# A two-block transformer kernel on one core: other places for the first weights, the turned input and the modulation groups in the opening order

## The reference, cut to what matters

```python
c_act = jax.nn.silu(c)
mod = (c_act @ ada_w[l] + ada_b[l]).reshape(B, N_MOD, D)[:, :, None, :]
shift_m, scale_m, gate_m, shift_f, scale_f, gate_f = [mod[:, i] for i in range(N_MOD)]
h = rmsnorm(x, norm_mix_g[l]) * (1.0 + scale_m) + shift_m
...
(p_q, p_k, p_v, p_g, p_gk, p_cq, p_ckv, p_kr, p_ga, p_gb) = jnp.split(h @ w_in, idx, axis=-1)
```

## Time and profile before

| | |
|---|---|
| three timed runs | 2636.22, 2636.57, 2638.76 us; median 2636.57 us |
| profiled execution, first to last instruction | span 2637.0 us |
| PE busy | 2552.6 us, 97% of the span |
| DVE busy | 1699.4 us, 64% |
| ACT busy | 1281.6 us, 49% |
| read from HBM | 549.83 MB |

### The profile page before, as it was taken

How to read it: one execution, slowest core, us unless ns; L and a number is a source line. 1 busy time by engine, 2 the same in 40 slices (tenths; PEclk the granted TensorE clock), 3 DMA queues, 4 the chain that set the end, 5 groups by cost and what they waited for, 6 DMA issues and landing times.

```text
span 2637.0 us, 33987 instructions
## 1 busy us (share of the span) xinstructions
PE 2552.6 (97%) x12327; PEld 2145.5 (81%) x12327; DVE 1699.4 (64%) x2194; ACT 1281.6 (49%) x1824; POOL 63.1 (2%) x102
## 2 busy tenths in 40 slices
PE   3889999999999999999999999999999999999999
PEld 3878887888887887888888888889888887888887
DVE  6887776776676765566655545565666655676664
ACT  3345455444555444544443444455754545565553
POOL 0000000000000000000000000000000100010000
PEclk9999999999999999999999999999999999999999
DMA  9975665898676665687756666566665465665564
GB/s 364 346 258 152 185 207 183 284 313 269 205 246 200 232 204 187 218 279 253 258 191 194 190 191 190 181 191 181 187 187 172 135 219 147 184 187 180 149 199 135
DMA packets 279920, 555.73 MB, mean 211 GB/s; under 512 B 24286, under 2 KB 45100, under 8 KB 279116
## 3 DMA queue, kind: packets, MB, share of 16 engines
q1 hardware_dynamic: 274048, 541.79, 64.6%
q0 software_dynamic: 3040, 8.69, 1.0%
q10 hardware_dynamic: 2668, 3.09, 0.3%
HBM read 549.83 MB, written 2.10 MB: 209 GB/s over the span
## 4 chain that ended last, share of the span: by engine, by line
PE 91%; DVE 4%; ACT 2%; issue 1%; DMA 1%; SPq 0%; POOL 0%; DVEq 0%; ACTq 0%
PE gp L830 83%; PE tp L830 5%; PE tp L833 2%; DMA raw_first<-in_ada_w_dram 1%; DVE wlo L1884 1%; ACT whi L1270 1%; DVE acc L1890 1%; DVE xs L1884 0%; SPq L813 0%; ACT hraw L1270 0%; DVE stat L2208 0%; ACT sx L1270 0%; DVE sx L1884 0%; DVE yd L1884 0%; ACT h L1270 0%
## 5 line engine op out<-in xcount | busy, mean ns | idle before, releaser
L1884 DVE TENSOR_TENSOR wlo<-raw,whi 128x1024 fp32r<-128x1024 f32 (+1 forms) x830 | 986.0, 1197 | 690.1 <-ACT whi L1270 687.4
L830 PE MATMUL gp<-whi,h 128*128 128x512 f32 (+1 forms) x4352 | 1371.4, 389 | 7.5 <-DVE wlo L1884 4.8
L1270 ACT ACTIVATE whi<-raw 128x1024 fp32r<-128x1024 f32 (+1 forms) x830 | 851.0, 1037 | 666.9 <-PE gp L830 545.6
L830 PEld LDWEIGHTS gp<-whi,h 128*128 128x128 f32 x4352 | 815.6, 188 | 165.9 <-issue 14.0
L830 PE MATMUL gp<-wlo,h 128*128 128x512 f32 (+1 forms) x2176 | 834.8, 384 | 0.0
L830 PEld LDWEIGHTS gp<-wlo,h 128*128 128x128 f32 x2176 | 409.9, 188 | 72.7 <-issue 1.7
L1890 DVE SCALAR_TENSOR_TENSOR acc<-raw,cact,acc 128x1024 f32<-128x1024 f32 x149 | 190.6, 1279 | 7.0 <-DMA raw<-in_ada_w_dram 6.2
L830 PE MATMUL gp<-whi,ah 128*128 128x512 f32 x352 | 137.9, 392 | 0.0
L830 PE MATMUL gp<-whi,al 128*128 128x512 f32 x352 | 137.1, 389 | 0.0
L830 PE MATMUL gp<-wlo,ah 128*128 128x512 f32 x352 | 136.9, 389 | 0.0
L830 PE MATMUL gp<-h,whi 128*128 128x256 f32 (+1 forms) x528 | 106.2, 298 | 20.9 <-ACT whi L1270 10.7
(11 more groups left out here) (331 smaller groups left out, 2593.7 us busy)
## 6 DMA issues: line engine op xcount, KB each, us to landing
raw<-in_w_in_dram SPq DMA_DIRECT2D x310, 512.0 KB, 4.3
raw<-in_ffn_w_in_dram SPq DMA_DIRECT2D x176, 512.0 KB, 4.5
raw<-in_ada_w_dram SPq DMA_DIRECT2D x158, 512.0 KB, 4.8
raw<-in_w_out_dram SPq DMA_DIRECT2D x96, 512.0 KB, 4.4
raw<-in_ffn_w_down_dram SPq DMA_DIRECT2D x88, 512.0 KB, 4.3
raw<-in_w_in_dram SPq DMA_DIRECT2D x64, 384.0 KB, 3.3
raw_first<-in_ada_w_dram SPq DMA_DIRECT2D x34, 512.0 KB, 8.4
raw<-in_gla_wo_dram SPq DMA_DIRECT2D x32, 512.0 KB, 5.8
```

The lines of the kernel that those rows point to most:

```text
L830: return e.matmul(o, l, r, start=start, stop=stop)
L1270: return e.activation(o, i, f, **kw)
L1884: return e.tensor_tensor(o, a, b, op)
```

## The change

It rewrites the order of the opening part; no arithmetic is added or removed.

- The first two weight chunks (q_0_0.0 and q_0_0.1) stand ahead of group 1 in `units`, at places 16 and 17 (before: 20 and 22).
- The 16 chunks of group 1 are spread over the first 0.8 of quarter 0's chunks, those of groups 2 and 3 over the first 0.85; the weight chunks are spread evenly over the whole (before: groups over the whole, weight chunks over the last 0.8). So each quarter begins with a weight chunk soon after its first ada chunk, and a group ends two or three weight chunks before its quarter's end (before: none or one).
- `x` is turned for quarter 0 at the end of stage `start`, ahead of group 0's `ada_mod` on PE. The norm of `x` (stage `start`) stands two chunks earlier.
- `fn_T` on ACT is split off as `fn_mod`, which stands in the same step as `fn_hi`, pair by pair. In quarters 1 to 3 the transposes stand one unit after `ada_mod` and one unit before `fn_mod`.
- At chunk 14 of the list the line is written out as far as quarter 0's `h`, ahead of every chunk of group 1 on ACT and DVE.

```diff
--- before.py
+++ after.py
@@ -250,8 +250,11 @@
     units = [(adas[0], ci) for ci in range(KD)]
     for qd in range(3):
         mine = [(job, ci) for job in quarters[qd] for ci in range(len(job["chunks"]))]
-        spots = [((i + 0.5) / 16, 0, u) for i, u in enumerate((adas[qd + 1], ci) for ci in range(KD))]
-        spots += [(0.2 + 0.8 * (i + 0.5) / len(mine), 1, u) for i, u in enumerate(mine)]
+        lead = mine[:2] if qd == 0 else []
+        units += lead
+        mine = mine[len(lead):]
+        spots = [((0.85 if qd else 0.8) * (i + 0.5) / 16, 0, u) for i, u in enumerate((adas[qd + 1], ci) for ci in range(KD))]
+        spots += [((i + 0.5) / len(mine), 1, u) for i, u in enumerate(mine)]
         units += [u for _, _, u in sorted(spots, key=lambda s: s[:2])]
     for job, ci in units + [(job, ci) for job in quarters[3] if job["kind"] != "v" for ci in range(len(job["chunks"]))]:
         job["chunks"][ci]["first"] = True
@@ -302,15 +305,14 @@
 
 def stage_steps(sid):
     kind, args = sid[0], sid[1:]
-    no = []
 
     def step(*parts, need=()):
         return (list(parts), list(need))
 
     idle = step()
     if kind == "start":
-        return [idle] * 2 + [step(("x_sq", (), 0)), step(("rows", (), 1))] + [idle] * 4 + [step(("x_ss", (), 0)), idle] + \
-            [step(("x_norm", (t,), 0)) for t in range(2)]
+        return [idle] * 2 + [step(("x_sq", (), 0)), step(("rows", (), 1)), idle, idle, step(("x_ss", (), 0)), idle] + \
+            [step(("x_norm", (t,), 0)) for t in range(2)] + [step(("fn_T", (0,), 1), ("fn_T", (1,), 1))]
     if kind == "adaf":
         (seq,) = args
         return [step(("ada_mod", (seq,), 1))]
@@ -319,8 +321,9 @@
         return [step(("ada_add", (seq, 0), 0), ("ada_add", (seq, 1), 0)), idle, idle, idle, step(("ada_out", (seq, 0), 1)), step(("ada_out", (seq, 1), 1))]
     if kind == "fnorm":
         (j,) = args
-        return [step(("fn_T", (2 * j,), 1), ("fn_T", (2 * j + 1,), 1), need=[("start",)]),
-                step(("fn_hi", (2 * j,), 0), ("fn_hi", (2 * j + 1,), 0), *([("gla_loads", (), 0)] if j == 3 else no))]
+        turn = [step(("fn_T", (2 * j,), 1), ("fn_T", (2 * j + 1,), 1))] if j else []
+        last = [("gla_loads", (), 0)] if j == 3 else []
+        return turn + [step(*[(part, (2 * j + n,), 0) for n in range(2) for part in ("fn_mod", "fn_hi")], *last)]
     if kind == "tables":
         return [step(("t_ang", (), 0)), step(("t_sin", (), 0)), idle, idle, step(("t_cos", (), 0)), step(("t_lam", (0,), 0)),
                 step(("t_lexp", (0,), 0), ("t_lam", (1,), 0)), step(("t_lexp", (1,), 0), ("t_cexp", (), 0)), step(("t_lfin", (0,), 0)),
@@ -507,7 +510,10 @@
             if not c["gemm"] and c["ci"] == KD - 1 and j["seq"] >= 4:
                 launch("ada", j["seq"])
             prep += 1
-        if job["kind"] == "ada" and ci == KD - 1 and job["seq"] < 4:
+        if n == KD - 2:
+            launch("adaf", 0)
+            until(("fnorm", 0))
+        if job["kind"] == "ada" and ci == KD - 1 and 0 < job["seq"] < 4:
             launch("adaf", job["seq"])
         if job["kind"] != "ada":
             kind, args = job["kind"], job["args"]
@@ -1389,10 +1395,10 @@
             copy(HH[:, 2 * pair:2 * pair + 2, :], hr[:, pair % 2, :, :]).then_inc(h_hi, 1)
             note(h_hi, "h", was, pair)
 
-        def fn_T(us, pair):
+        def fn_mod(us, pair):
             m = first_use("ada_mod", pair // 2)
             w.wait_ge(tp_dve[m.b], at("tpd", *m))
-            norm_T(us[0], pair, hraw, 1, 0, "h")
+            norm_T(first_use("fn_T", pair), pair, hraw, 1, 0, "h")
 
         def fn_hi(us, pair):
             norm_hi(first_use("fn_T", pair), pair, hraw, "h")
...
```

More of the change, by code:

```diff
@@ L1867, in after_dve @@
                     note(ss_done, "ss", "dn", j, n)
-        parts = dict(rows=rows, x_sq=x_sq, x_norm=x_norm, prep=prep, ada_out=ada_out, fn_T=fn_T, fn_hi=fn_hi, t_sin=t_sin,
+        parts = dict(rows=rows, x_sq=x_sq, x_norm=x_norm, prep=prep, ada_out=ada_out, fn_mod=fn_mod, fn_hi=fn_hi, t_sin=t_sin,
                      t_lexp=t_lexp, t_cexp=t_cexp, t_cln=t_cln, gk_la=gk_la, gk_ln=gk_ln, gk_kr=gk_kr, gk_krt=gk_krt, gla_sum=gla_sum, gla_exp=gla_exp,
```

## The result

The changed kernel took **2647.18 us** (median of 5 runs, 2644.35 to 2647.55) against 2636.57 us for the kernel before (median of 5, 2635.99 to 2639.16). The ratio is **1.0031**, 95% interval 1.0021 to 1.0042: slower by 0.31%. The profiled execution has a span of 2642.5 us and took 2644.35 us; the one of before has 2637.0, so the two traces are 5.5 us apart. The timed medians are 10.6 us apart; the traces can explain only their own 5.5.

A forecast was written before the change was run, and what follows sets the result against it. PE and DVE were taken as level in the opening quarters, so work DVE skips at borders returns as PE waits. Start's gain lost, +0.7 at quarter 2, +5.8 at gk, not won back: 2642 us, range 2633 to 2647.

The forecast's parts named there:

- The start: Up to the first matmul: norm earlier, POOL's table loads delay the last chunks; 46.1 us against 48.85, -2.75 us.
- Quarter 0's waits: PE waits while DVE does two or three ada chunks between weight chunks: 6.7 us against 2.76 before.
- warm, PE just waits longer: Behind the borders: whether the clock falls is left open, since a full-clock PE would only wait longer for DVE.
- Quarter 1: 28 DVE slots of 1.17 us from 92.2 to 125.2; quarter 2 then starts at 141.3, +0.7 us against before.
- behind both borders DVE sets the pace and PE waits for it anyway: After the borders into quarters 1 and 2: DVE is the limit, so a lower PE clock need not be costed.
- Quarter 2: Tables' chain delays q_1_2.0's subtraction to 150.9, 3.9 us late; gk product starts at 203.6 against 197.84, +5.8 us.
- Rival (b): Quarter 2: the sine's chain is hidden, 1.8 us and one ada chunk fall away; +2.5, 2639 us; chance 0.25.
- an engine that is behind doesn't wait: Quarter 2, DVE from q_1_2.0's to v_2_2.1's subtraction: 34.9 us without a wait taken, not 36.7 with before's waits.
- After gk: Behind the gk product: the 5.8 us aren't won back; 99.06 of 102.16 us busy, every engine in the old order.
- Rival (a): Quarters 0 to 2: borders were the price and DVE has slack enough; -9.9 less 3.9, 2630.5 us; chance 0.15.
- Rival (c): The start: early tables stop everything, `ada_mod` and `modc` go beyond 44.5 us; +9, 2646 us; chance 0.1.
- The page against the row: DVE slots, 56 in all: skill page's whole durations give 1.25 us, 2646 to 2647; forecast uses the rows' 1.17.

The follow-up runs named there:

- pool_late: Changed kernel with POOL's four table loads held until the first low half of `h` is written; 2644.32 us, ratio 1.0024 to the kernel before.
- early_h_tables_late: Changed kernel with `fn_mod` and `fn_hi` moved into the transposes' step and the tables launched beside quarter 2's last v block; 2629.79 us, ratio 0.9964 to before.
- list_only: Kernel before with only the new list of chunks, its stages kept; 2641.92 us, ratio 1.0010 to the kernel before.
- tables_late: Changed kernel with the tables launched beside quarter 2's last v block, not when its `h` is made; 2639.27 us, ratio 1.0001 to the kernel before.
- early_h: Changed kernel with `fn_mod` and `fn_hi` in the transposes' step, ahead of ACT's evacuation; 2637.01 us, ratio 0.9995 to the kernel before.
- light_after: Changed kernel with sums of groups 1 to 3, from each second chunk on, over 8 of 1024 columns; 2631.87 us, ratio 0.9977 to the kernel before.
- best_again: Repeat of the changed kernel with both early `fn_mod`/`fn_hi` and late tables; 2629.30 us, ratio 0.9962 to the kernel before.

## Why the prediction came out as it did

Forecast: 2642 us, 0.2% slower, with a range up to 2647. Measured: 2647.18, 0.31% slower, at the very edge of that range; the trace 2642.5 for 2642.8. The mechanism is the one forecast: DVE, level with PE, owes the sums that it did not do while `h` was made. That the trace fits to 0.3 us is luck in part. At gk it is 0.2 us from the forecast, and this is made of misses that cancel: -0.9 at the first matmul, -0.8 in quarter 0, +1.1 in quarter 1, +0.4 in quarter 2. The steps:

- **The start**, -2.75 us forecast, -3.61 measured. The six traces with the same opening have the first matmul at 46.1 on average, as forecast, so the surplus is that of one trace. The tables fell on the last chunks as said (2.06 us before the last ada chunk, q_0_0.1 landed at 39.87 for 40.9); `mk` was issued at 29.29 and not near 31.2, since POOL's power instruction started 4.1 us earlier instead of 3.1 and took 0.69 us for 1.64. `pool_late` gives the bound for no tables, 43.74 for 43.8.
- **Quarter 0's waits**, 6.7 us forecast, four waits of 4.65 us in the changed kernel. The pattern was right: `early_h_tables_late`, whose clock stayed up, has five waits of 0.67, 0.62, 2.01, 0.62 and 2.00 us (5.92) where 0.8, 0.8, 2.2, 2.2 and 0.65 were forecast:

```profile
57.86 0.36 PE L836 MATMUL gp<-h,whi 128*128 128x256 f32 x1 [0.67 <-DVE wlo L1890]
61.59 0.35 PE L836 MATMUL gp<-h,whi 128*128 128x256 f32 x1 [0.62 <-DVE wlo L1890]
...
66.69 0.35 PE L836 MATMUL gp<-h,whi 128*128 128x256 f32 x1 [2.01 <-DVE wlo L1890]
70.42 0.36 PE L836 MATMUL gp<-h,whi 128*128 128x256 f32 x1 [0.62 <-DVE wlo L1890]
...
75.53 0.35 PE L836 MATMUL gp<-h,whi 128*128 128x256 f32 x1 [2.00 <-DVE wlo L1890]
```

  In the changed kernel the clock fell at 65.4, after the wait of 2.01 us, and PE's slower units ate the next 0.62 and 0.65 us of waiting. From the matmul behind the wait of 2.01 us to the second one behind it (64.98 to 73.81, 66.69 to 75.53) it is 8.83 us in the one and 8.84 in the other: here the lower clock cost nothing, and "warm, PE just waits longer" held. Without the border the quarter is 39.89 us in one and 40.60 in the other, where the faster pace set in 2 us later behind the first matmul. Against the 6.7 us forecast the five waits were 0.8 us shorter in all. The border was 3.56 for 3.5, so the quarter took 43.45 for 44.3.
- **Quarter 1**: its end was close (v_1_1.1's subtraction at 124.61 for 125.2, quarter 2 at 140.71 for 141.3) only because it began 1.7 us early. Its length was 52.02 us for 50.9, and this is the step that failed: "behind both borders DVE sets the pace and PE waits for it anyway". DVE did not run through. From q_0_1.1's subtraction to v_1_1.1's it took 34.17 us for 33.0. It has two idle times at the quarter's start, the larger one on PE's cold product:

```profile
90.44 1.23 DVE L1890 TENSOR_TENSOR wlo<-raw,whi 128x1024 fp32r<-128x1024 f32 x1 [0.33 <-ACT whi L1276]
96.19 1.29 DVE L1890 TENSOR_TENSOR qt<-gp,qt 128x512 f32<-128x512 f32 x2 [0.99 <-PE gp L836]
```

  In quarters 1 and 2 DVE adds finished products, so a slow PE holds DVE, and the time is lost to both. Of the 1.1 us that the quarter was too long, this idle time is at most 0.99; `list_only`, at full clock, still has 0.57 of it, and `early_h_tables_late` has no idle time of DVE between 88 and 128 us. In quarter 0 ACT copies the products, and DVE does not wait for them; that this is why the same sentence held there is argued, not shown.
- **Quarter 2**: 62.69 us for 62.3. The subtraction at 150.37 for 150.9, a wait of 3.62 within the 3 to 5 said, v_2_2.1's subtraction at 185.62 for 185.8 (35.25 us for 34.9), gk at 203.40 for 203.6. Rival (b), the hidden sine, is out. The 34.9 us came out for the reason given, "an engine that is behind doesn't wait": DVE is busy for 34.69 of the 35.25 us, and its one idle time of note is on a cold product of PE:

```profile
160.35 1.29 DVE L1890 TENSOR_TENSOR qt<-gp,qt 128x512 f32<-128x512 f32 x2 [0.45 <-PE gp L836]
```

  The stretch at the lower clock, 6.8 us from 150.8 on, was not in the forecast, and it cost about half a microsecond here: `list_only`, with 3.4 us of it there and no such idle time, takes 34.71 us from the one subtraction to the other. By DVE's rows most of the 2.67 us that PE is busy beyond `tables_late` stood in the place of waits. Rival (b)'s price for the tables, 1.8 us and a chunk, is that of the sine's wait; `tables_late` also moves DVE's own work on the angles, 3.76 us ahead of q_1_2.0's subtraction, and so wins 6.5 us in the quarter.
- **After gk**: nothing won back, as forecast: 5.56 us at gk, 5.5 at the end.
- **Rival (a)**, borders as the price and slack on DVE, had one half right. Removing the borders' waits is worth 7.8 us at gk (`early_h`); the change did not remove them, it made them 1.0 and 2.0 us shorter and no more. The slack wasn't there: the sums cost 9.1 us (`light_after`). **Rival (c)** is out: `modc` at 42.29, before the 44.5 it needed.
- **The page against the row**: the slots stayed at the rows' pace, from 90.44 to 124.61 us 28 of them in 34.17, less 0.99 idle, 1.185 us each. The Trainium skill, "VectorE: DVE Perf Modes", section "The DRAIN you can't avoid", taken with the whole durations of 1.25 us, would have put gk some 3.6 us later than by this pace, an estimate; the trace does not agree with that reading. The same section adds that a next instruction that is not held starts earlier, and this the trace bears out: independent ones start before the record of the former ends.

What stays open: the timed medians differ by 5 us more than the traces. About 2.2 us of this are the kernel before's trace, slower than its median, and 2.8 the changed kernel's, the quickest of its five. More time at the lower clock does not explain the slower four: their mean granted clock is 0.995, that of the profiled one 0.994. No second trace of the changed kernel was taken, so what its slower executions lose isn't known.

## What to carry to other kernels

When two engines are level, an earlier start of the one is worth only what the other has in store; count the second engine's instructions that stand ahead, and look for its idle time while the first chain runs. On an engine that issues in order, put the chain that opens the next stage ahead of an evacuation that waits for the last matmul of this one: here that took 3.56 us from each of two borders and with it the cold stretches behind them. A side job's place (the tables) has to be chosen again after each change of the order around it: the same edit was worth 6.5 us of quarter 2 in the new order and cost 1.1 in the old.

## What the runs showed of the hardware

- In the opening the matmuls' pace went from one 128x256 matmul in 0.21 us to one in 0.12 at 3.1 us (changed kernel, at 48.4), 3.7 (`list_only`, 50.2), 4.1 (before, 53.0), 5.2 (`early_h_tables_late`, 51.2), 4.6 (`best_again`, the same kernel, 51.0) and 5.8 us (`pool_late`, 49.5) after the first long matmul. The clock column of the windows view reads 1.00 before that point too.
- The granted clock fell within or right behind each of the changed kernel's idle times of 3.56, 3.57 and 3.62 us. After `list_only`'s 2.51 us it did not fall at 89.17 but did after the equal ones that ended at 138.71 and 148.70 us, and in the changed kernel it fell at 65.4 within busy matmuls after waits of 0.67, 0.62 and 2.01 us. With the same waits it did not fall in `early_h_tables_late` and did in `best_again`, the same kernel. So the length of one idle time does not decide it, and neither does the program.
- What 3.4 us at the lower clock cost depended on which engine set the pace there: 1.43 us where PE had no waits (`pool_late`, 12.75 us for 11.32), nothing where DVE had none (quarter 0, 8.83 us for 8.84), and 0.4 to 1.0 us where DVE added PE's products (quarter 1).
- DVE starts an independent 128x1024 instruction 1.14 to 1.20 us after the last one, whose record is 1.22 to 1.28 us long, and an accumulation into the `acc` of the one just before it 1.39 us after that one.
